# Local attention: who rounds the rotated queries, and how the rotation is spread over the units

## The reference, cut to what matters

```
qb = q.reshape(B, nb, BLOCK, ATTN_KV_HEADS, ATTN_GROUP, ATTN_HEAD_DIM)   # 16 heads of 64, blocks of 128
kb, vb = bands(k), bands(v)                                             # own block and its neighbours
scores = jnp.einsum('bnqhgd,bnkhd->bnhgqk', qb, kb) * (ATTN_HEAD_DIM ** -0.5)
scores = jnp.where(mask, scores, NEG)                                   # |distance| <= 128
m = jnp.maximum(jnp.max(scores, axis=-1, keepdims=True), s)             # s: a sink per head
p = jnp.exp(scores - m)
probs = p / (jnp.sum(p, axis=-1, keepdims=True) + jnp.exp(s - m))
out = jnp.einsum('bnhgqk,bnkhd->bnqhgd', probs, vb)
```

## Time and profile before

| what | value |
|---|---|
| median of 3 runs | 3459.86 us (3459.03 to 3462.6) |
| the profiled execution | 3465.15 us |
| its span | 3463.3 us |
| TensorE busy | 3390.4 us, 98% of the span |
| VectorE, ScalarE, GpSimd busy | 57%, 35%, 36% |
| mean granted clock of TensorE | 0.994 of full speed |

### The profile page before, as it was taken

The page is one execution under the profiler, slowest core; times in us unless marked ns, Lnnn a source line. Parts: engine busy times, 40 slices in busy tenths (PEclk is TensorE's granted clock), DMA queues, the critical chain, the costliest instruction groups (busy, mean ns, idle before and its releaser), DMA issues.

```text
span 3463.3 us, 43097 instructions
## 1 busy us (share of the span) xinstructions
PE 3390.4 (98%) x16026; PEld 2793.4 (81%) x16026; DVE 1962.1 (57%) x2418; ACT 1218.6 (35%) x2092; POOL 1245.6 (36%) x800
## 2 busy tenths in 40 slices
PE   8989999999999999999999999999999999999999
PEld 7778888788888887777878888888788888878887
DVE  6666662844444476885284444447746546544455
ACT  6447761422222245764132222225434233102011
POOL 1120113444544440023344554444335344323340
PEclk9999999999999999999999999999999999999999
DMA  5010012111111122111211111112111111111241
GB/s 212 22 40 17 23 57 85 49 49 49 49 49 49 49 91 79 45 41 62 85 49 49 49 49 49 49 49 88 68 61 49 51 63 43 59 46 66 89 149 67
DMA packets 67635, 211.85 MB, mean 61 GB/s; under 512 B 7280, under 2 KB 11888, under 8 KB 65680
## 3 DMA queue, kind: packets, MB, share of 16 engines
q1 hardware_dynamic: 56848, 165.04, 14.3%
q10 hardware_dynamic: 10624, 44.63, 3.6%
HBM read 186.32 MB, written 22.02 MB: 60 GB/s over the span
## 4 chain that ended last, share of the span: by engine, by line
PE 89%; DVE 5%; ACT 2%; issue 2%; POOL 1%; DMA 1%; ACTq 0%; DVEq 0%; SPq 0%; POOLq 0%
PE G L860 36%; PE G L1276 20%; PE AUX L1228 16%; PE G L1518 3%; PE G L1099 2%; PE AUX L1397 2%; PE AUX L1295 2%; PE AUX L1161 2%; PE AUX L1151 1%; PE G L982 1%; PE AUX L1141 1%; PE AUX L1028 1%; PE AUX L1479 1%; POOL slot_lo L709 1%; PE AUX L1009 0%
## 5 line engine op out<-in xcount | busy, mean ns | idle before, releaser
L860 PE MATMUL G<-Hhi,whi 128*128 128x512 f32 x1552 | 631.6, 407 | 7.4 <-DVE Hlo L2629 2.8
L860 PE MATMUL G<-Hhi,wlo 128*128 128x512 f32 x1552 | 605.4, 390 | 0.0
L860 PE MATMUL G<-Hlo,whi 128*128 128x512 f32 x1552 | 605.1, 390 | 0.0
L674 POOL CAST whi<-wraw 128x1024 fp32r<-128x1024 f32 (+1 forms) x123 | 136.8, 1112 | 1293.2 <-PE G L860 599.9
L1276 PE MATMUL G<-u_hi,slot_hi 128*128 128x512 f32 x1024 | 401.9, 393 | 6.4 <-DVE X L2584 5.1
L1276 PE MATMUL G<-u_lo,slot_hi 128*128 128x512 f32 x1024 | 399.7, 390 | 0.0
L1276 PE MATMUL G<-u_hi,slot_lo 128*128 128x512 f32 x1024 | 399.6, 390 | 0.0
L860 PEld LDWEIGHTS G<-Hhi,whi 128*128 128x128 f32 x1552 | 292.3, 188 | 74.3 <-issue 7.1
L2583 DVE TENSOR_TENSOR G<-G,r 128x1024 f32<-128x1024 f32 x128 | 157.8, 1232 | 332.8 <-PE G L1276 332.6
L709 POOL TENSOR_TENSOR slot_lo<-raw_down,slot_hi 128x512 fp32r<-128x512 f32 x144 | 191.1, 1327 | 423.1 <-ACT slot_hi L1898 422.9
L860 PEld LDWEIGHTS G<-Hlo,whi 128*128 128x128 f32 x1552 | 292.3, 188 | 62.7 <-issue 5.7
(11 more groups left out here) (453 smaller groups left out, 6836.2 us busy)
## 6 DMA issues: line engine op xcount, KB each, us to landing
wraw<-wjobs SPq DMA_DIRECT2D x148, 512.0 KB, 3.4
raw_down<-down_pairs SPq DMA_DIRECT2D x64, 512.0 KB, 3.3
raw_up<-up_units SPq DMA_DIRECT2D x30, 512.0 KB, 3.6
raw_up<-up_units SPq DMA_DIRECT2D x44, 256.0 KB, 3.2
mw_raw<-wjobs SPq DMA_DIRECT2D x16, 512.0 KB, 5.2
scratch<-X ACTq DMA_DIRECT2D x2, 4096.0 KB, 13.2
gate_tiles<-gate_st ACTq DMA_DIRECT2D x16, 512.0 KB, 4.4
T<-gate_tiles ACTq DMA_DIRECT2D x16, 512.0 KB, 3.4
```

The source lines that it names most:

```text
L674: pool.tensor_copy(whi[:, par, 0:kt], wraw[:, par, 0:kt]).then_inc(w_hi, 1)
L860: mm = pe.matmul(G[:, par if psum is None else psum, cols], w[:, par, k, :], x[:, k, cols], start=(i == 0 and j == 0), stop=(i == kt - 1 a ...
```

## The change

GpSimd casts the rotated queries of pairs 1 to 7 in place of ScalarE. It does the two heads one after the other, each behind a wait on the one before. Pair 0 stays with ScalarE. VectorE's five operations of a half are no longer done in two places (three and two) but in four: partners·sin (`partner`), then q·cos and the sum (`rotate`), then the low part of the first head, then that of the second (`head`). The first of the four stands where the rotation stood, for most halves; the other three follow at the next three units. GpSimd's queue is written out: `queries_high(p, 0)`, the split of one weight job, `queries_high(p, 1)`.

```
-        turning = {1: ((1, 4, 6, 8), (6, 9, 11, 13)), KT - 1: tuple(
-            tuple(16 * (KT - 2) + u for u in at) for at in ((4, 6, 7, 8), (12, 14, 15, 16)))}
+        turning = {1: ((1, 4, 5, 7, 8), (6, 9, 10, 12, 13)), KT - 1: tuple(
+            tuple(16 * (KT - 2) + u for u in at) for at in ((4, 6, 7, 8, 9), (12, 14, 15, 16, 17)))}
         for p in range(2, KT - 1):
-            turning[p] = tuple(tuple(16 * (p - 1) + u for u in at) for at in ((8, 10, 11, 12), (16, 18, 19, 20)))
-        raw_at, rotate_at, high_at, low_at = (
-            {at[step]: (p, c) for p, halves in turning.items() for c, at in enumerate(halves)} for step in range(4))
+            turning[p] = tuple(tuple(16 * (p - 1) + u for u in at) for at in ((8, 10, 11, 12, 13), (16, 18, 19, 20, 21)))
+        raw_at, partner_at, rotate_at, first_low_at, second_low_at = (
+            {at[step]: (p, c) for p, halves in turning.items() for c, at in enumerate(halves)} for step in range(5))
...
-            splits(START["k"], START["wo_mixed0"])
-            split(START["wo_mixed0"], START["wo_mixed0"] // 2, 0, True)
+            def queries_high(p, c):
+                pool.wait_ge(q_rot, 2 * p + c + 1)
+                for h in range(2):
+                    at = slice(h * HD, (h + 1) * HD)
+                    pool.tensor_copy(QS[p % 2][at, h, c * 512:(c + 1) * 512], rotating[at, :]).then_inc(q_hi, 1)
+                    pool.wait_ge(q_hi, 4 * p + 2 * c + h + 1)
+            splits(START["k"], START["q"] + 2)
+            split(START["q"] + 2, START["q"] // 2 + 1, 0, True)
+            for p in range(1, KT):
+                queries_high(p, 0)
+                if p < KT - 1:
+                    split(START["q"] + p + 2, (START["q"] + p + 2) // 2, p % 2, True)
+                queries_high(p, 1)
...
-                    if v in high_at:
-                        queries_high(*high_at[v])
...
+                def partner(p, c):
+                    cols = slice(c * 512, (c + 1) * 512)
+                    dve.wait_ge(swapped, 32 * (2 + 2 * p + c + 1))
+                    return chain.mark(dve.tensor_tensor(Q[p % 2][:, 1, cols], partners[:], sin[:, cols], ALU.mult))
+                def rotate(p, c, turned):
+                    cols = slice(c * 512, (c + 1) * 512)
+                    q0, q1 = (Q[p % 2][:, n, cols] for n in range(2))
                     chain.link(dve.tensor_tensor(q0, q0, cos[:, cols], ALU.mult))
+                    chain.wait(turned)
                     dve.tensor_tensor(rotating[:], q0, q1, ALU.add).then_inc(q_rot, 1)
+                def head(p, c, h):
+                    dve.wait_ge(q_hi, 4 * p + 2 * c + h + 1)
...
+                    low = dve.tensor_tensor(QS[p % 2][other, h, cols], rotating[part, :], QS[p % 2][part, h, cols],
+                                            ALU.subtract)
+                    if h == 0:
+                        chain.link(low)
+                    else:
+                        low.then_inc(rot_ok, 1)
...
+                    if v in partner_at:
+                        turned = partner(*partner_at[v])
                     if v in rotate_at:
-                        rotate(*rotate_at[v])
-                    if v in low_at:
-                        heads(*low_at[v])
+                        rotate(*rotate_at[v], turned)
+                    if v in first_low_at:
+                        head(*first_low_at[v], 0)
+                    if v in second_low_at:
+                        head(*second_low_at[v], 1)
```

More of the change, by code:

```diff
@@ L2476, in window @@
                        .then_inc(vcopied, 1)
-                def rotate(p, c):
+                def partner(p, c):
[3 more added lines that the diff above has]
+                def rotate(p, c, turned):
                     cols = slice(c * 512, (c + 1) * 512)
                     q0, q1 = (Q[p % 2][:, n, cols] for n in range(2))
-                    dve.wait_ge(swapped, 32 * (2 + 2 * p + c + 1))
-                    chain.link(dve.tensor_tensor(q1, partners[:], sin[:, cols], ALU.mult))
                     chain.link(dve.tensor_tensor(q0, q0, cos[:, cols], ALU.mult))
+                    chain.wait(turned)
                     dve.tensor_tensor(rotating[:], q0, q1, ALU.add).then_inc(q_rot, 1)
-                def heads(p, c):
[L2489 to L2500, removed]
+                def head(p, c, h):
+                    dve.wait_ge(q_hi, 4 * p + 2 * c + h + 1)
+                    cols = slice(c * 512, (c + 1) * 512)
+                    part, other = slice(h * HD, (h + 1) * HD), slice((1 - h) * HD, (2 - h) * HD)
+                    low = dve.tensor_tensor(QS[p % 2][other, h, cols], rotating[part, :], QS[p % 2][part, h, cols],
[4 more added lines that the diff above has]
+                        low.then_inc(rot_ok, 1)
+                def heads(p, c):
+                    head(p, c, 0)
+                    head(p, c, 1)
+                rotate(0, 0, partner(0, 0))
                 heads(0, 0)
@@ L2531, in window @@
                 peak(1)
-                rotate(0, 1)
+                rotate(0, 1, partner(0, 1))
                 for v in range(U):
```

## The result

The changed kernel takes 3472.22 us in the median of 8 runs (3469.49 to 3475.36); the kernel before took 3463.4 us in 8 runs beside it (3459.03 to 3466.94). The ratio is 1.0027, with a 95% interval of 1.0016 to 1.0038. A second series, further down, gave 3470.97 against 3464.13 us, 1.0027 (1.0017 to 1.0037). So the change costs 7 to 9 us, where 1.6 us were forecast, and the time lies above the range. Of the distance to the forecast of 3461.5 us, 3.5 us are the base: the three runs that it started from had a median of 3459.86 us, and 33 runs of the same kernel in a later series have one of 3463.31 us. The other 7.2 us are what the change did beyond the forecast.

What follows compares the result with a forecast made beforehand. The prediction took TensorE, 89% of the chain, as the bound, with only its idle time to save. Terms +5.1 − 4.0 − 0.7 − 0.8 + 2.0 = +1.6 us on 3459.9 gave 3461.5 us, range 3454.5 to 3470 (8 in 10).

Steps and rivals of the forecast that it cites:

- The mechanism of the stall: Units 5 and 13: turn, peak, second low part and the next scores become one serial chain, so scores waits.
- The stalls: Ten halves of pairs 1 to 6: scores later by 4 × 0.64 + 0.71 + 5 × 0.37 = +5.1 us.
- The 0.8 us are gone: Unit 5, second halves: without ScalarE's casts ahead of the exp, turn(5) comes when TensorE is ready, saving 0.8 us.
- Pairs 0 and 1: Stage start: the split no longer delays partners·sin, fewer casts on ScalarE; −4.0 us, bounds −1.5 and −5.5.
- Pair 7: First half −0.7 us; second half −0.8 us, bounds −2.5 and +0.5, its split running late beside the low parts.
- Ties with GpSimd: Ten halves of pairs 2 to 6: second cast ties with scale_out's first operation; 0 to +5.7 us, taken as +2.0.
- The stalls simply go: Rival: second low part done in time for scores, ten 0.8 us losses saved; −13.5 us, 3446 us; 10%.
- The shared port decides: Rival: GpSimd wins every tie and late splits hold VectorE in pairs 0 and 7; +9.1 us, 3469 us; 10%.
- TensorE's clock falls: Rival: second halves' five longer waits lower the clock, each costing about half of 6.5 us; +17.6 us, 3477 us; 7%.

Runs made afterwards that it cites:

- the tables alone: Changed kernel's spread VectorE places, but casts on ScalarE at the first low part's unit and GpSimd's splits as before: 3468.81 us, ratio 1.0017 to the kernel before.
- last version: Changed kernel, four places one unit earlier, last split before last casts, first-low-part wait moved before the second, pair 1's split after turn(16): 3445.03 us, ratio 0.9945.
- the early split: Changed kernel with GpSimd's last weight split put ahead of the casts of pair 7's second half: 3465.48 us, ratio 1.0004 to the kernel before.

## Why the forecast was wrong, step by step

**The mechanism of the stall was right.** "What is late next is the second low part", behind `peak(7)`: `scores` waits where the forecast put it, and the runs with the tables alone and with the low parts moved back show that it is this. One link is not the one named: `turn(5)` ended 0.51 us before `peak(7)` started, and what held the peak was VectorE itself, with the first low part and the wait behind it. What failed in the sum are two terms above all: the stalls, which were too small, and pair 7, which had the wrong sign.

**The stalls: +8.3 us, not +5.1.** Per half, +0.85 in place of +0.64 in second halves (pairs 2 to 5), +1.03 in place of +0.71 in pair 6, and +0.71 in place of +0.37 in first halves, and +0.35 more in pair 4. The forecast made the peak follow the low part within 0.03 us. The change has VectorE wait there for its own result, which was in the diff (`chain.link(low)`) and was not priced: 0.18 us a half, shown by the run without it. The second low part, too, starts 0.03 us after the end of line 2534 (334.77, 334.80), where the forecast let the two overlap by 0.08. The two make 0.29 a half, 2.9 us in ten halves, and the ten halves without pair 4's extra are 8.0 − 5.1 = 2.9 us over the forecast. That the sums meet is partly chance: in the second halves of pairs 2 to 5 the first low part stood 0.1 us earlier in its unit than forecast (1.23 us after the unit's start, 1.33 before), and in the first halves the 0.1 us of `scale_out` behind the first cast are in the 0.71.

**"The 0.8 us are gone": they are, but not for the reason given.** The forecast gave the whole to the casts on ScalarE. With the casts alone moved, `turn(5)` still waited 0.22 us; with the spreading alone and the casts still on ScalarE (one unit later) it did not wait. And an unhindered `turn(5)` is worth little as long as the low parts come right behind it: the two versions with both low parts in their old unit left unit 5 at 2.78 and 2.89 us.

**Pairs 0 and 1: −4.0 forecast, −5.7 and −2.1 in two executions,** once the 0.7 us of stall in pair 1 is taken out. Their mean is near the forecast, but with a spread of 3.6 us that is luck. The part that was worked out from rows did hold: `turn(7)` came 17.97 us after the stage's first `scores` (236.83 and 218.86), before 21.09, so −3.1 where −2.8 was forecast. The two executions differ by the clock: the second one had it at the low level for 13.7 us from 240 us on, the first not at all in these pairs (the kernel before had 6.8 and 10.2 us of it). The collision of the split with the low parts and `scale_out` was forecast, and is there:

```profile
239.30 2.69 POOL L676 TENSOR_TENSOR wlo<-wraw,whi 128x1024 fp32r<-128x1024 f32 x1
...
240.71 1.29 DVE L2540 TENSOR_TENSOR wstat<-wstat 128x2 f32<-128x2 f32 x1
```

An operation of 0.15 us took 1.29, and `turn_result` waited 1.52 us for it. Putting that split off (last version) made pair 0 shorter by 1.15 us, 31.87 to 30.72.

**Pair 7: the −0.8 us of its second half came out as +1.0 to +2.1. This is the step with the wrong sign.** The −0.7 us of its first half did come, in pair 6, where unit 9 fell from 2.82 to 2.15 us. For the second half the forecast saw that the split would wait behind the casts, and placed it at "463 to 467, beside the low parts". It gave that collision a bound of +0.5 us, although had priced it: an operation of 128x512 caught by `wlo` lasts until about half a microsecond after it. It was the last low part, 2.83 us in place of 0.69, and the next peak and `turn_result` came late with it. With the split out of the way the pair takes 35.6 us: the change would have saved 2.6 us here, the low clock of the kernel before included.

**Ties with GpSimd: +0.5, not +2.0.** The forecast read one tie off a second half and gave it to all ten halves at 0.57 us each when lost. In the second halves of pairs 2 to 5 the two did start together and VectorE lost nothing; in pair 6 `scale_out` came after the casts. In the five first halves `scale_out` met the first cast, near its end, and lost 0.1 us each, which the run without casts on GpSimd shows (3.55 us in place of 3.65). These 0.5 us are contained in the 8.3 above. It is a matter of 0.1 us where VectorE's operation falls: in the version with everything one unit earlier it was the low part that was caught, at 0.44 us a time.

**The rivals.** "The stalls simply go" fell with the ten waits. "The shared port decides" came nearest with its +9.1, by luck: its 5.7 us of ties were 0.5, and the port's price lay mainly in pair 7. "TensorE's clock falls" was right in part: after waits of 1.8 us in pair 4 it fell in three of four executions (the changed kernel's first, the early split, the spreading alone) and not in the fourth; after the waits of 1.47 and 1.41 us in other pairs it never did.

**What the medians add.** In the second series the kernel before had 8 runs of 3458.05 to 3460.25 us with a mean granted clock of 0.996 to 0.997, and 11 of 3464.05 to 3465.02 at 0.994; the 11 further runs lie between 3459.53 (0.996) and 3467.39 (0.993). The changed one had 5 runs of 3468.78 to 3470.97 at 0.995 and 4 of 3473.36 to 3475.5 at 0.993 to 0.994. At 0.994 the two are 9 us apart, the medians 7, and the stage gave 5.5 and 6.3. What is left lies outside the stage, where the two programs do the same work: behind it the changed kernel was 1.6 and 3.9 us longer in the two pairs of executions, and its clock stood low there for 28.5 and 28.4 us in all, against 24.9 and 21.4. The parts outside the stage differ between executions in the steps of such stretches: ahead of it 218.9 and 214.6 us for one and the same changed kernel, with 10.2 us and none at the low level. None of its 17 runs reached 0.996. Whether its waits bring more such stretches, behind the stage too, was not tried and is open.

## What to carry to other kernels

Before moving an operation one step later, write out the chain from what frees it to what needs it, with every wait on the engine's own last result in it, and compare it with the whole time between the two. Here two low parts of 0.69 us did no harm side by side, and cost 0.8 us a half with a peak between them. When work is put ahead of other work on GpSimd, follow the displaced work to the place where it now runs and list VectorE's operations there; one split of 3.8 us at the end of the stage cost 4.7 us with the clock that fell behind it, more than half of the 8.3 us of the ten stalls. And move the whole group by a unit before giving up the idea: the same spreading, one unit earlier, with its splits placed and one wait moved, was 0.55% faster than the kernel before, by 16.0 us in the stage and some more by the clock.

## What the runs showed of the hardware

- A VectorE wait for its own previous result, with nothing else late, cost 0.18 us a time; at one instruction, in the same place in four executions, it was 0.57 us between the two operations in place of 0.21. The cause of the latter is open.
- Two GpSimd casts of 64x512 take 1.28 to 1.31 us with the gap between them. One alone takes 0.60 or 0.61 us, and 0.64 where `scale_out` began with it (at 332.34 us in the changed kernel). That is as long as one of 128x512, 0.613 in the earlier trace rows: half the partitions saved nothing.
- A VectorE operation with two inputs in SBUF that began during GpSimd's work took 2.83 us for 0.69 and 1.29 us for 0.15 beside `wlo`, and 1.13 us for 0.69 and 0.24 us for 0.15 beside a cast. Each of them ended about its own length less 0.14 us after GpSimd's instruction did: 0.54 us (`partners·sin` of the earlier trace rows, 0.68 long) and 0.55 us (the low parts, 0.69 long), and 0.01 to 0.02 us (`scale_out`, 0.15 long).
- Which of the two began first decided who was held. In the version with everything one unit earlier the low part took 1.13 us when the cast had begun 0.03 us before it, and in the first halves, where the low part was first, the cast took 1.13 us in place of 0.61.
- TensorE's granted clock stands low for stretches of 3.4 to 13.7 us, and one of 3.4 us costs 1.6 us. The same program, in two executions, had most of them at the same places and some in one execution alone, and the changed kernel's 9 runs of the second series lie 6.7 us apart. The last version had four of 3.4 us beside the one at the very end, none of them in the stage, and its 5 runs lie within 1.2 us.
